# Output phase of a hybrid layer on Trainium2: product groups and small TensorE steps in a mixed order, column sums folded on GpSimd

## The chip, the cores and the metric

The kernel runs on one core of a Trainium2 chip. The metric is the device time of one launch in microseconds (us). A core has TensorE (PE), VectorE (DVE), ScalarE (ACT), GpSimd (POOL) and SyncE (SP, which here issues the DMA transfers). Each engine works through its own instructions in order; semaphores order the engines among each other.

## The reference, cut to what matters

The layer has eight phases, one after the other, each a block of its own: modulation, input projection, recurrence, attention, output, routing, experts, combination. Only the output phase is changed. For each of 2048 tokens it computes:

```python
o  = concat([rms_norm(r * gelu(g), gn_rnn), rms_norm(a, gn_attn)]) @ w_out   # 512 + 512 -> 1024
x1 = layer_norm(alpha * x + g1 * o, ln1_g, ln1_b)                            # post-norm
h2 = modulate(x1, shift, scale)                                              # second layer norm, scaled and shifted
logits = h2 @ [router_g, router_e] + bias                                    # 36 columns
```

`x1` and `h2` go to HBM for the later phases, the logits stay in SBUF. The gains `gn` and the gate `g1` are multiplied into the weight. The root mean square of each half is taken of its token, so it is applied to the finished product of that half, one factor per token for each.

## The kernel before, in words

The tokens are 16 tiles (`T_LAT`) of 128. The recurrence half arrives transposed (`yT`, 128 channels by 4 blocks of 128 tokens), the attention half by rows (`at`); TensorE transposes the latter. For float32 accuracy with float16 products every operand is split into a high and a low float16 part, and three products are summed: high x high, high x low, low x high (L1416 to L1418). One tile takes 8 groups `k` of 6 such matmuls (128x128 weights, 512 columns): groups 0 to 3 sum the recurrence half in PSUM banks 2 and 3, groups 4 to 7 the attention half in banks 4 and 5.

At the start ScalarE rounds the weight to `whi` in 8 pieces (L1349), VectorE computes `wlo` (L1284), and TensorE starts when all 8 are there (L1387). Then `tiles` (L1193) gives each engine the same order of steps; step `t` is

- `project(t)`: TensorE's 48 product matmuls;
- `normalise(t - 1)`: ScalarE scales the recurrence half (L1373, to `t0`), VectorE adds the other half and the residual (L1312, L1314) and does two layer norms (L1315 to L1338), in which GpSimd twice raises a variance to the power -0.5 (L1275) while VectorE waits;
- `prepare(t + 1)`: ScalarE squares both halves (L1355, L1358) and rounds them (L1361 `yhi`, L1363 `ahi`), VectorE computes the low parts (L1292 `ylo`, L1294 `alo`), TensorE transposes the attention half (L1394) and sums the squares of the recurrence half over the channels by four matmuls with a column of ones (L1401), ScalarE copies that sum (L1365), VectorE scales it (L1298) and GpSimd takes the power (L1269);
- `route(t - 2)`: TensorE transposes `h2` in 8 blocks (L1428), ScalarE evicts them in two halves (L1381), TensorE multiplies by the router (8 float32 matmuls of 36 columns, L1434), VectorE adds the bias (L1342).

`yhi`, `ylo`, `ahi` and `alo` have one buffer each, so their writers wait until the products of the tile before have ended (`o_mm`, L1360 and L1291). The column sums lie in bank 0, which the transposes of `h2` write too: these wait for ScalarE's copy of the sum (L1424). SyncE loads `yT` and `at` of tile `t + 2` when the parts of tile `t` are made, stores `x1` and `h2` of tile `t`, and loads `x` (`xt`) of tile `t + 2`. `link` (L1305) makes VectorE wait for each own instruction; `v` counts 14 per tile.

## Time and profile before

| | us |
|---|---|
| median of 3 runs | 2208.11 |
| lowest, highest | 2204.58, 2208.21 |
| profiled execution, its span | 2208.1 |
| output phase, first ScalarE instruction to last logits | 848.5 to 1158.0 |
| busy over the whole span | PE 84%, DVE 68%, ACT 47%, POOL 18% |

The span is the profiled execution's own time; nothing of it lies outside. Starts are in us from the start of the span. The output phase lies in slices 16 to 21 of the page's 40. A matmul's duration includes its way through the array, so matmuls overlap, and what one costs is the distance to the next start. In the lists "xN" is the number of instructions merged into a row, and a bracket gives the engine's idle time just before it and what ended that.

### The profile page before, as it was taken

To read this page: it belongs to the slowest core of one execution; us is meant where nothing else is said; L and a number is where in the kernel's file an instruction comes from. 1 tells how busy PE (TensorE), PEld (TensorE's weight loads), DVE (VectorE), ACT (ScalarE), POOL (GpSimd) and SP (SyncE) were. 2 spreads that over 40 slices of the span, in tenths; PEclk is the share of its full clock that TensorE was granted. 3 is DMA by queue.
4 is the path that set the end of the run, shared out by engine and by line. 5 is a ranking of instruction groups with operands and counts; after the bars stand their busy time and mean duration, and the time that the engine had idled before them with its cause. 6 is when DMAs were issued, how large, how long until landed. Compare 5 with 4: busy or idle time off the path is not lost. (4 is left out here: it accounts for less than half of the span.)

```text
span 2208.1 us, 41507 instructions
## 1 busy us (share of the span) xinstructions
PE 1847.0 (84%) x11836; PEld 1047.0 (47%) x11837; DVE 1498.4 (68%) x1859; ACT 1036.7 (47%) x1360; POOL 388.5 (18%) x375
## 2 busy tenths in 40 slices
PE   2488988889489996999971799999999988989946
PEld 0066666534277774555540345455444444445422
DVE  2357676388789995777669626656758888765537
ACT  1044434577478885222210514544646766543326
POOL 0000000000012211222212112222322323222213
PEclk7689999999799997988975799999999999999979
DMA  9712121276351111333323738778879999986637
GB/s 369 290 58 96 57 85 58 106 246 230 134 196 57 62 52 58 124 114 122 124 77 118 267 67 282 221 225 291 295 230 375 377 370 379 329 285 179 213 83 266
DMA packets 167722, 417.63 MB, mean 189 GB/s; under 512 B 16160, under 2 KB 24768, under 8 KB 163952
## 3 DMA queue, kind: packets, MB, share of 16 engines
q1 hardware_dynamic: 152832, 362.87, 44.9%
q0 software_dynamic: 14832, 54.01, 10.0%
q8 instruction: 34, 0.56, 0.1%
q14 instruction: 24, 0.20, 0.0%
HBM read 343.39 MB, written 73.45 MB: 189 GB/s over the span
## 5 line engine op out<-in xcount | busy, mean ns | idle before, releaser
L1946 PE MATMUL ps<-arena 128*128 x1200 | 459.3, 383 | 43.3 <-DVE arena L1866 43.1
L1866 DVE SCALAR_TENSOR_TENSOR arena<-arena 128x2048 f32 (+1 forms) x186 | 421.1, 2289 | 107.3 <-ACT arena L1810 49.9
L1947 PE MATMUL ps<-arena 128*128 x1200 | 458.9, 382 | 0.0
L1948 PE MATMUL ps<-arena 128*128 x1200 | 458.5, 382 | 0.0
L1804 ACT ACTIVATE arena<-arena 128x2048 f32 (+1 forms) x124 | 233.2, 1908 | 154.1 <-DMA arena<-w 67.9
L618 PE MATMUL ps<-arena 128*128 128x256 f16 (+1 forms) x1680 | 237.7, 303 | 21.1 <-DVE arena L503 21.1
L618 PEld LDWEIGHTS ps<-arena 128*128 128x128 f16 x1680 | 165.8, 100 | 87.3 <-DVE arena L503 15.2
L1946 PEld LDWEIGHTS ps<-arena 128*128 128x128 f16 x1200 | 118.1, 98 | 185.2 <-issue 59.5
L1948 PEld LDWEIGHTS ps<-arena 128*128 128x128 f16 x1200 | 118.4, 99 | 140.7 <-issue 4.5
L1947 PEld LDWEIGHTS ps<-arena 128*128 128x128 f16 x1200 | 118.1, 98 | 131.8 <-issue 4.0
L1810 ACT ACTIVATE arena<-arena 128x2048 f32 (+1 forms) x62 | 117.4, 1908 | 68.7 <-DMA arena<-w 50.6
L1866 DVE SCALAR_TENSOR_TENSOR arena<-ps,arena 128x512 f16<-128x512 f32 (+1 forms) x101 | 96.4, 954 | 70.4 <-ACT arena L1827 44.2
L1105 DVE CUSTOM_DVE_ANT_0 arena<-ps,arena,small 128x640 f32<-128x640 f32 x128 | 112.8, 881 | 14.4 <-PE ps L1047 5.5
L1047 PE MATMUL ps<-arena 128*128 (+3 forms) x768 | 94.0, 259 | 28.9 <-DMA arena<-qT_d 28.1
L1416 PE MATMUL ps<-arena 128*128 128x512 f16 x256 | 109.0, 426 | 2.9 <-ACT arena L1373 2.9
L1817 ACT ACTIVATE arena<-ps 128x1024 f16<-128x1024 f32 x51 | 52.0, 1019 | 122.8 <-PE ps L1941 122.8
L1059 PE MATMUL ps<-idn,arena 128*128 128x128 f32 x640 | 93.5, 277 | 18.8 <-ACT arena L1138 9.7
L1417 PE MATMUL ps<-arena 128*128 128x512 f16 x256 | 108.7, 425 | 0.0
L1418 PE MATMUL ps<-arena 128*128 128x512 f16 x256 | 107.9, 421 | 0.0
L1138 ACT ACTIVATE arena<-arena,small 128x640 f32<-128x640 f32 x128 | 105.0, 820 | 6.2 <-DVE small L1105 6.2
L1147 ACT ACTIVATE arena<-ps 128x640 f16<-128x640 f32 x128 | 90.1, 704 | 35.7 <-PE ps L1078 30.9
L1111 DVE SCALAR_TENSOR_TENSOR arena<-ps,arena 128x640 f16<-128x640 f32 x128 | 104.8, 819 | 1.9 <-ACT arena L1147 1.9
(287 smaller groups left out, 3040.5 us busy)
## 6 DMA issues: line engine op xcount, KB each, us to landing
arena<-w SPq DMA_DIRECT2D x186, 1024.0 KB, 12.9
arena<-hT_d SPq DMA_DIRECT2D x64, 512.0 KB, 6.0
arena<-w_mod SPq DMA_DIRECT2D x12, 2048.0 KB, 17.2
h_d<-arena SPq DMA_DIRECT2D x17, 512.0 KB, 3.0
x_d<-arena SPq DMA_DIRECT2D x17, 512.0 KB, 2.6
arena<-x SPq DMA_DIRECT2D x8, 1024.0 KB, 6.3
hT_d<-arena SPq DMA_DIRECT2D x16, 512.0 KB, 3.7
arena<-x SPq DMA_DIRECT2D x16, 512.0 KB, 4.7
```

The lines of the kernel that those rows point to most:

```text
L618: mm = pe.matmul(o, lhs, rhs, start=first and n == 0, stop=last and n == 2)
L1105: nc.vector.tensor_tensor_reduce(b[f"s{m % 4}"], scores_at(m), b[f"mask{j}"], -undo, neg_sink[:, h:h + 1], ALU.add, ALU.min, nm[j][:, h:h ...
L1138: nc.scalar.activation(b[f"s{m % 4}"], b[f"s{m % 4}"], ACT.Exp, bias=nm[j][:, h:h + 1], scale=-1.0, accum_out=den[j][:, h:h + 1]).then_inc ...
L1416: pe.matmul(o, lhs_hi, whi[:, k0 + k, cols], start=(k == 0), stop=False)
L1417: pe.matmul(o, lhs_hi, wlo[:, k0 + k, cols], start=False, stop=False)
L1418: mm = pe.matmul(o, lhs_lo, whi[:, k0 + k, cols], start=False, stop=(k == C_RNN - 1))
L1804: nc.scalar.activation(part(buf, whi, n * PIECE, PIECE), b["st"][:, n * PIECE:(n + 1) * PIECE], ACT.Copy, scale=W_SCALE).then_inc(hi13, 1)
L1810: nc.scalar.activation(part(buf, whi, n * PIECE, PIECE), b["st"][:, n * PIECE:(n + 1) * PIECE], ACT.Copy, scale=W_SCALE).then_inc(hi2, 1)
L1866: return nc.vector.scalar_tensor_tensor(dst, src, scale, high, ALU.mult, ALU.subtract)
L1946: pe.matmul(out, high, part(buf, whi, at, 512), start=first, stop=False)
L1947: pe.matmul(out, high, part(buf, wlo, at, 512), start=False, stop=False)
L1948: return pe.matmul(out, low, part(buf, whi, at, 512), start=False, stop=last)
```

## The change

TensorE's small steps are put between the 8 product groups, and the two halves get semaphores of their own (`o_y`, `o_mm`). A step `t` of TensorE is now: group 0, transposes of `at` (t + 1), group 1, first half of the transposes of `h2` (t - 2), group 2, second half, column sum (t + 1), groups 3 and 4, first half of the router's matmuls (t - 2), group 5, second half, groups 6 and 7. GpSimd adds the four blocks of squares to one (`fold`, two additions of 256 and 128 columns), so that one matmul into bank 7 does the column sum. `yhi`, `ylo`, `ahi` and `alo` get two buffers each. VectorE computes the low parts of tile t + 1 and adds the router's bias between an instruction of `normalise` and its wait for GpSimd's power. TensorE waits for each piece of the split weight by itself, and tile 0 is prepared between the 4th and 5th piece. SyncE loads both first pairs of `yT` and `at` ahead of `xt`, and refills one tile further ahead. `fold_d` reuses a semaphore of the first phase, whose count is already 1.

```diff
-    b = arena_slices(arena[:, 0:OUT_W0], 0, [("logits", T_LAT * 36), ("ones", 1), ("mh", 2), ("ysq", 512), ("asq", 512)]
-                     + [(n, 256) for n in ("yhi", "ylo", "ahi", "alo")]
+    b = arena_slices(arena[:, 0:OUT_W0], 0, [("logits", T_LAT * 36), ("ones", 1), ("mh", 2), ("ysq", 512), ("ysum", 128), ("asq", 512)]
+                     + [(f"{n}{j}", 256) for n in ("yhi", "ylo", "ahi", "alo") for j in range(2)]
...
+            def refill(t, j):
+                sp.wait_ge(lo, START + 2 * t + 2)
+                sp.sem_inc(g["alone"], 1)
+                sp.wait_ge(sq, START + 2 * t + 2)
+                sp.sem_inc(g["alone"], 1)
+                load_in(t + 2, j)
+
+            refill(0, 0)
+            for t in range(T_LAT):
+                if t + 3 < T_LAT:
+                    refill(t + 1, 1 - t % 2)
+                stores(t, t % 2)
+                if t + 2 < T_LAT:
+                    load_x(t + 2, t % 2)
...
+            def fold(t):
+                pool.wait_ge(sq, START + 2 * t + 1)
+                pool.sem_inc(g["alone"], 1)
+                pool.wait_ge(ssm, START + t)
+                pool.sem_inc(g["alone"], 1)
+                nc.gpsimd.tensor_tensor(b["ysq"][:, 0:2 * P], b["ysq"][:, 0:2 * P], b["ysq"][:, 2 * P:4 * P], ALU.add).then_inc(fold_d, 1)
+                pool.wait_ge(fold_d, START + 2 * t + 1)
+                pool.sem_inc(g["alone"], 1)
+                nc.gpsimd.tensor_tensor(b["ysum"], b["ysq"][:, 0:P], b["ysq"][:, P:2 * P], ALU.add).then_inc(fold_d, 1)
+
+            def first():
+                fold(0)
+                prepare(0, 0)
+
+            def step(t, j):
+                if has_next(t):
+                    fold(t + 1)
+                if known(t, 1):
+                    normalise(t - 1, 1 - j)
+                if has_next(t):
+                    prepare(t + 1, 1 - j)
+            tiles(pool, first, step, lambda: normalise(T_LAT - 1, 1))
...
                 link(nc.vector.scalar_tensor_tensor(t1, t1, mv[:, 0:1], b["l1g"], ALU.subtract, ALU.mult))
+                if while_first is not None:
+                    while_first()
                 dve.wait_ge(pw, START + 2 * t + 1)
...
                 link(nc.vector.scalar_tensor_tensor(x1n, x1, mv[:, 0:1], b["sc2"], ALU.subtract, ALU.mult))
+                if while_second is not None:
+                    while_second()
                 dve.wait_ge(pw, START + 2 * t + 2)
...
+            def first():
+                nc.vector.tensor_scalar(b["sc2"], b["sc2"], 1.0, None, ALU.add).then_inc(w_ok, 1)
+                for k in range(C_RNN):
+                    split_w(k)
+                low_y(0, 0)
+                low_a(0, 0)
+                squares(0, 0)
+                for k in range(C_RNN, KD):
+                    split_w(k)
+                dve.wait_ge(w_ok, START + 1)
+
+            def step(t, j):
+                def first_wait():
+                    if has_next(t):
+                        low_y(t + 1, 1 - j)
+
+                def second_wait():
+                    if has_next(t):
+                        low_a(t + 1, 1 - j)
+                    if known(t, 2):
+                        route(t - 2)
+                if known(t, 1):
+                    normalise(t - 1, 1 - j, first_wait, second_wait)
+                else:
+                    first_wait()
+                    second_wait()
+                if has_next(t):
+                    squares(t + 1, 1 - j)
+
+            def finish():
+                normalise(T_LAT - 1, 1)
+                route(T_LAT - 2)
+                route(T_LAT - 1)
...
             def prepare(t, j):
                 act.wait_ge(in_ld[j], START + 32 * half(t) + 32)
 
-                act.wait_ge(ssm, START + t)
+                act.wait_ge(fold_d, START + 2 * t)
                 nc.scalar.activation(b["ysq"], b[f"yT{j}"], ACT.Square).then_inc(sq, 1)
 
-                act.wait_ge(ssv_d, START + t)
+                if known(t, 2):
+                    act.wait_ge(o_y, START + t - 1)
+                nc.scalar.activation(yhi[j], b[f"yT{j}"], ACT.Copy, scale=X_SCALE).then_inc(hi, 1)
+
+                if known(t, 2):
+                    act.wait_ge(ssv_d, START + t - 1)
+                act.wait_ge(sq, START + 2 * t + 1)
                 nc.scalar.activation(b["asq"], b[f"at{j}"], ACT.Square, accum_out=ss[j][:, 1:2]).then_inc(sq, 1)
-
-                act.wait_ge(o_mm, START + t)
-                nc.scalar.activation(yhi, b[f"yT{j}"], ACT.Copy, scale=X_SCALE).then_inc(hi, 1)
                 act.wait_ge(a_tr, START + t + 1)
-                nc.scalar.activation(ahi, ps[:, 6, :], ACT.Copy, scale=X_SCALE).then_inc(hi, 1)
+                if known(t, 2):
+                    act.wait_ge(o_mm, START + t - 1)
+                nc.scalar.activation(ahi[j], ps[:, 6, :], ACT.Copy, scale=X_SCALE).then_inc(hi, 1)
                 act.wait_ge(ssm, START + t + 1)
-                nc.scalar.activation(ss[j][:, 0:1], ps[:, 0, 0:1], ACT.Copy).then_inc(ss_d, 1)
-
-            def normalise(t, j):
-                act.wait_ge(o_mm, START + t + 1)
+                nc.scalar.activation(ss[j][:, 0:1], ps[:, 7, 64:65], ACT.Copy).then_inc(ss_d, 1)
+
...
+            def first():
+                for k in range(C_RNN):
+                    high_w(k)
+                prepare(0, 0)
+                for k in range(C_RNN, KD):
+                    high_w(k)
+
+            def step(t, j):
+                if has_next(t):
+                    prepare(t + 1, 1 - j)
+                if known(t, 2):
+                    route(t - 2)
+                scaled(t, j)
...
+            def column_sums(t):
+                pe.wait_ge(fold_d, START + 2 * t + 2)
+                pe.wait_ge(ss_d, START + t)
+                if known(t, 4):
+                    pe.wait_ge(lg, START + t - 3)
+                pe.matmul(ps[:, 7, 64:65], b["ysum"], b["ones"], start=True, stop=True).then_inc(ssm, 1)
+
+            def product(t, j, k):
+                bank, high, low, at = (2, yhi[j], ylo[j], k) if k < C_RNN else (4, ahi[j], alo[j], k - C_RNN)
+                if at == 0:
+                    pe.wait_ge(lo, START + 2 * t + (1 if bank == 2 else 2))
 
                     if bank == 2:
                         pe.wait_ge(o_act, START + t)
-                    elif not isinstance(t, int) or t > 0:
+                    elif known(t, 1):
                         pe.wait_ge(v, START + NV * t - NV + 1)
-                    for k in range(C_RNN):
-                        for n in range(2):
-                            o, cols = ps[:, bank + n, :], slice(n * 512, (n + 1) * 512)
-                            lhs_hi, lhs_lo = high[:, k * P:(k + 1) * P], low[:, k * P:(k + 1) * P]
-                            pe.matmul(o, lhs_hi, whi[:, k0 + k, cols], start=(k == 0), stop=False)
-                            pe.matmul(o, lhs_hi, wlo[:, k0 + k, cols], start=False, stop=False)
-                            mm = pe.matmul(o, lhs_lo, whi[:, k0 + k, cols], start=False, stop=(k == C_RNN - 1))
-                mm.then_inc(o_mm, 1)
-
-            def route(t, j):
-                pe.wait_ge(v, START + NV * t + 14)
-
-                pe.wait_ge(ss_d, START + t + 4 if not isinstance(t, int) else START + min(t + 4, T_LAT))
-                pe.wait_ge(h_ev, START + 2 * t)
+                if not known(t, 1):
+                    pe.wait_ge(w_lo, START + k + 1)
...
+            def router(t, n):
+                pe.wait_ge(h_ev, START + 2 * t + n + 1)
+
+                if n == 0:
+                    pe.wait_ge(lg, START + t)
+                    pe.wait_ge(ss_d, START + (min(t + 4, T_LAT) if isinstance(t, int) else t + 4))
...
+            def first():
+                pe.wait_ge(p_ok, START + 2)
+                transposes_a(0, 0)
+                column_sums(0)
+
+            def step(t, j):
+                product(t, j, 0)
+                if has_next(t):
+                    transposes_a(t + 1, 1 - j)
+                product(t, j, 1)
+                if known(t, 2):
+                    transposes_h(t - 2, j, 0)
+                product(t, j, 2)
+                if known(t, 2):
+                    transposes_h(t - 2, j, 1)
+                if has_next(t):
+                    column_sums(t + 1)
+                product(t, j, 3)
+                product(t, j, 4)
+                if known(t, 2):
+                    router(t - 2, 0)
+                product(t, j, 5)
+                if known(t, 2):
+                    router(t - 2, 1)
+                product(t, j, 6)
+                product(t, j, 7)
+
+            def finish():
+                for t in (T_LAT - 2, T_LAT - 1):
+                    for n in range(2):
+                        transposes_h(t, t % 2, n)
+                    for n in range(2):
+                        router(t, n)
```

## Rows read from the trace of the kernel before

**Rows 1.** The page's slices: granted TensorE clock, tenths of full speed.
```profile
PEclk7689999999799997988975799999999999999979
```

**Rows 2.** Waits in the output phase, 880 to 1125: us in total, times, longest.
```profile
ACT arena L1361 <- PE ps L1418: 118.8, 14, 11.3
...
DVE arena L1342 <- PE ps L1434: 39.4, 13, 3.4
```

**Rows 3.** TensorE in time over one step: start, length, line, shape, count, idle before.
```profile
974.78 0.60 PE L1394 MATMUL ps<-idn,arena 128*128 128x128 f32 x4
975.22 0.95 PE L1401 MATMUL ps<-arena 128*128 128x1 f32 x8
976.51 1.09 PE L1428 MATMUL ps<-idn,arena 128*128 128x128 f32 x8 [0.34 <-ACT small L1365]
978.41 1.97 PE L1434 MATMUL ps<-arena 128*128 128x36 f32 x16 [0.81 <-ACT arena L1381]
980.21 0.38 PE L1416 MATMUL ps<-arena 128*128 128x512 f16 x1
...
984.06 0.38 PE L1417 MATMUL ps<-arena 128*128 128x512 f16 x1
...
992.26 0.60 PE L1394 MATMUL ps<-idn,arena 128*128 128x128 f32 x4
```

**Rows 4.** Attention, and one output step: us, busy per engine, PEclk, DMA.
```profile
680.00:720.00 40.00, 36.53 (x574) 30.93 (x573) 37.16 (x70) 33.57 (x70) 10.79 (x11) 1.00 0.19 64
974.78:992.26 17.48, 16.33 (x85) 9.15 (x84) 12.60 (x19) 4.62 (x9) 3.90 (x4) 0.90 0.35 120
```

**Rows 5.** ScalarE in time: the first act behind a tile's products, twelve steps apart.
```profile
903.54 0.63 ACT L1361 ACTIVATE arena<-arena 128x512 f16<-128x512 f32 x1 [4.85 <-PE ps L1418]
...
1116.18 0.63 ACT L1361 ACTIVATE arena<-arena 128x512 f16<-128x512 f32 x1 [8.41 <-PE ps L1418]
```

**Rows 6.** VectorE in time over one step.
```profile
909.11 0.20 DVE L1342 TENSOR_TENSOR arena<-ps,arena 128x36 f32 x1 [1.86 <-PE ps L1434]
909.22 1.27 DVE L1312 SCALAR_TENSOR_TENSOR arena<-ps,small,arena 128x1024 f32<-128x1024 f32 x1
...
915.70 1.29 DVE L1325 SCALAR_TENSOR_TENSOR arena<-arena,small 128x1024 f32<-128x1024 f32 x1 [0.61 <-POOL small L1275]
...
920.71 1.29 DVE L1338 SCALAR_TENSOR_TENSOR arena<-arena,small 128x1024 f32<-128x1024 f32 x1 [0.53 <-POOL small L1275]
922.20 0.69 DVE L1292 SCALAR_TENSOR_TENSOR arena<-arena 128x512 f16<-128x512 f32 x1 [0.21 <-ACT arena L1363]
922.81 0.68 DVE L1294 SCALAR_TENSOR_TENSOR arena<-ps,arena 128x512 f16<-128x512 f32 x1
```

**Rows 7.** GpSimd by line and shape: count, busy us, mean ns.
```profile
L1027 POOL TENSOR_TENSOR arena<-arena 128x1024 f32 x8 | 19.0, 2371 | 2.8 <-DMA arena<-router 2.8
...
L1269 POOL TENSOR_TENSOR small<-small,arena 128x2 f32<-128x2 f32 x16 | 11.3, 704 | 73.8 <-DVE small L1298 73.8
```

**Rows 8.** The line L1105 alone: duration ns min, median, max.
```profile
L1105 DVE CUSTOM_DVE_ANT_0 arena<-ps,arena,small x128: 873/883/886, 611.2 to 838.4; 128x640 f32<-128x640 f32 x128
```

**Rows 9.** The phase's start: DVE, SP and PE in time.
```profile
849.76 9.66 DVE L1284 SCALAR_TENSOR_TENSOR arena<-arena 128x1024 f16<-128x1024 f32 x8 [0.56 <-ACT arena L1349]
...
848.90 0.50 SPq L1227 DMA_DIRECT2D arena<-attn_d  x1
...
859.52 1.09 PE L1394 MATMUL ps<-idn,arena 128*128 128x128 f32 x4 [14.45 <-DVE arena L1284]
...
861.96 0.59 PE L1416 MATMUL ps<-arena 128*128 128x512 f16 x1
```

**Rows 10.** DMA issues, 847 to 862: KB each, median us to landing.
```profile
arena<-attn_d SPq DMA_DIRECT2D x2, 256.0 KB, 4.9
```

**Rows 11.** First tile's end (875.27), and the phase's end, in time.
```profile
875.27 0.60 PE L1394 MATMUL ps<-idn,arena 128*128 128x128 f32 x4
...
1135.00 1.04 PE L1428 MATMUL ps<-idn,arena 128*128 128x128 f32 x8
...
1138.97 1.27 DVE L1312 SCALAR_TENSOR_TENSOR arena<-ps,small,arena 128x1024 f32<-128x1024 f32 x1
...
1157.84 0.20 DVE L1342 TENSOR_TENSOR arena<-ps,arena 128x36 f32<-128x36 f32 x1 [6.15 <-PE ps L1434]
```

More of the change, by code:

```diff
@@ L1191, in phase_output, with tiles @@
     NV = 14
-    def tiles(eng, prepare, project, normalise, route):
-        def step(t, j, first=False, second=False, last=False):
-            project(t, j)
-            if not first:
-                normalise(t - 1, 1 - j)
-            if not last:
-                prepare(t + 1, 1 - j)
-            if not first and not second:
-                route(t - 2, j)
-        prepare(0, 0)
-        step(0, 0, first=True)
-        step(1, 1, second=True)
+    def tiles(eng, first, step, finish):
+        first()
+        step(0, 0)
+        step(1, 1)
         with eng.Fori(1, T_LAT // 2 - 1) as i:
@@ L1209, in tiles, with known, has_next @@
         step(T_LAT - 2, 0)
-        step(T_LAT - 1, 1, last=True)
-        normalise(T_LAT - 1, 1)
-        route(T_LAT - 2, 0)
-        route(T_LAT - 1, 1)
-    def none(t, j):
-        pass
+        step(T_LAT - 1, 1)
+        finish()
+    def known(t, low):
+        return not isinstance(t, int) or t >= low
+    def has_next(t):
+        return not isinstance(t, int) or t + 1 < T_LAT
     def half(t):
@@ L1439, with finish @@
+            def finish():
+                for t in (T_LAT - 2, T_LAT - 1):
[3 more added lines that the diff above has]
+                        router(t, n)
+            tiles(pe, first, step, finish)
 W13 = 2 * KD * D_EXP
```

98 lines of the change are left out of this document (47 added, 51 removed).

## The prediction

> **What bounds the kernel now.** The change touches the output phase only, so I read that stage and not the whole span. The page's slices come first: in the 16th to 21st slice, 828 to 1159 us, the granted TensorE clock is 7, 9, 8, 8, 9 and 7 tenths, where the four slices of attention before them have 9 [rows 1]. Then the waits of the stretch: the longest is ScalarE's, 118.8 us for the end of a tile's products, and VectorE's is 39.4 us for the router's matmuls [rows 2]; TensorE waits little. So TensorE's own sequence sets the step. Third, TensorE in time [rows 3], read by the distances of starts, since the lengths overlap:
>
> - transposes of `at`: 974.78 to 975.22, 0.44 us, 0.11 each;
> - column sums (8 passes in 0.95) and the wait for ScalarE's copy (0.34): to 976.51, 1.29 us;
> - transposes of `h2` and the wait for ScalarE's eviction (0.81): to 978.41, 1.90 us;
> - router: to 980.21, 1.80 us;
> - 48 products: to 992.26, 12.05 us. The last 38 of them, from 984.06, take 8.20 us, 0.2158 each; the first ten take 3.85 us where 2.16 would do. The clock has gone to its lower level (1.2 GHz) behind the small steps and comes back after 3.4 us: 1.69 us lost.
>
> Together 17.48 us. Over twelve steps ScalarE's marker moves from 903.54 to 1116.18, 17.72 us a step [rows 5]; the 0.24 more is steps in which the low level lasts longer. VectorE is busy 12.6 us of a step, ScalarE 4.6, GpSimd 3.9, and the clock is 0.90 [rows 4].
>
> **The new step on TensorE.** 48 products at 0.2158: 10.36. Transposes of `at` 0.44. Column sum: 2 passes in place of 8, 0.22. Transposes of `h2`: 8 at 0.11, 0.88. Router 1.80. Sum 13.70; a step now returns five times from float32 pieces to products, before once. No row shows a return by itself (that behind the router is inside its 1.80, for 16 passes, 0.11 each, as for the transposes), so I bound one by 0 and 0.1 and take 0.1 for all: 13.8 us. That holds if both waits go and the clock stays up.
>
> The waits: the transposes of `h2` no longer share bank 0 with the sum, and between each transposition and its use stand two to three groups of 1.29 us, for ScalarE's copy and two evictions. The router's first half comes 2.6 us behind the column sum; ScalarE needs a copy and one eviction in that time, and is busy 4.6 us of a step in all [rows 4]. No wait is left there.
>
> The clock: attention's TensorE stream is a mix of transposes and short matmuls at 91% busy (36.53 of 40 us), and has 1.00 [rows 4]. The new step has no idle gap, and no small piece longer than 0.9 us between products. I take 1.00.
>
> **The other engines.** VectorE becomes the nearest rival. From L1312 at 909.22 to the end of L1338 at 920.71 + 1.29 = 922.00 a `normalise` takes 12.78 us [rows 6]. Two waits for GpSimd lie in it, 0.61 and 0.53. In the first goes `low_y` (0.61 from start to start), at no cost; in the second `low_a` (about 0.6) and the router's bias (0.11 to the next start), 0.2 more than the gap. The scaling of the squares (0.16) and the waits at the step's end add 0.4. That is 13.4 us, below 13.8, so TensorE still sets the pace, by 0.4 us only. The bias add waits for the router's second half, at 6 x 1.29 + 0.44 + 0.88 + 0.22 + 1.80 = 11.1 us of TensorE's step; VectorE comes to it at 920.71 - 0.53 - 909.22 = 11.0, plus 0.6 for `low_a`, 11.6. Behind it are queued L1338 and the next tile's normalisation; TensorE needs that `h2` only two steps on.
>
> GpSimd: nothing here shows a 256-column addition. 1024 columns of the same kind take 2371 ns, 2 columns of a power 704 [rows 7]. By columns the fold is 384/1024 of 2371, 0.9 us, plus a start for each and the wait between them: 1.3 us. Its bounds are 0.9 and 2 x 2.37 = 4.7. It starts when the power of tile t is done, about 0.8 us into TensorE's step, and the column sum needs it at 5.2 (three groups, all transposes but none of the router). So up to 4.4 us cost nothing; at 4.7 TensorE would stand 0.3 us a step. The power for `normalise` is asked for as L1321 starts, 915.70 - 0.61 - 1.28 - 909.22 = 4.6 us behind L1312 [rows 6], when a fold of 1.3 us is long over.
>
> The fold runs beside L1312 and L1314. L1105 has a maximum of 886 ns against a median of 883 over 128 instances [rows 8], though eight of GpSimd's 2.4 us multiplications ran in that stretch [rows 7]: no slowing. It reads one operand from PSUM, however, and L1314 has both in SBUF. The Trainium skill ("GPSIMD Engine Reference", section 8, Key points) says that GpSimd shares its SBUF interfaces with VectorE, with contention where a VectorE instruction has two SBUF inputs. By that rule L1314 could stretch; the rows don't show that case, and it is a rival below.
>
> SyncE: its transfers keep size and number; `yT` and `at` are now issued one step earlier, 13 us or more ahead of use.
>
> **The start.** Before, TensorE waits for the eighth low piece (849.76 + 9.66 = 859.42), and the first product starts at 861.96 [rows 9]. Now four pieces (VectorE at 854.6) and tile 0's parts are enough. `at` of tile 0 is issued at 848.90 and lands 4.9 us later [rows 9, 10], 853.8; square 0.6, fold 1.3, the column sum at the low clock 0.4: the first product at 856.1, 5.8 us earlier. Tile 0's products then include tile 1's transposes and sum, 1.2 us at the low clock. The end of tile 0 moves from 875.27 [rows 11] to 875.27 - 5.8 + 1.2 = 870.7. The later low pieces come every 1.2 us and are ahead of groups of 1.3 to 2.6 us.
>
> **The sum.** Step 1 has no `h2` yet: 11.0 us, to 881.7. Steps 2 to 14: 13 x 13.8 = 179.4, to 1061.1. Step 15 has no next tile: 13.1, to 1074.2. Before, that point is 1135.00 [rows 11]. The last `normalise` no longer waits for a router product (before it starts 4.0 us behind, at 1138.97), but VectorE gets to it just then, 1074.3. From there to the last logits nothing changes: 1138.97 to 1158.04 is 19.1 us [rows 11], so 1093.4 in place of 1158.0. The gain is 64.6 us: 4.6 at the start, 56.2 in the steps, 3.8 at the end. The profiled execution has 2208.1 us, the same as the median of the runs, so 2208.1 - 64.6 = 2143.5, say 2144 us.
>
> **The rivals.**
>
> - *VectorE sets the pace.* For: only 0.4 us of room, more waits of its own, and L1314 beside the fold. If L1314 (1.2 us) doubled, a step is 14.6: 0.8 x 13 = 10 us, 2154. Against: L1105 is unmoved [rows 8]. 18%.
> - *The clock still falls.* TensorE goes back and forth between float16 groups and float32 pieces five times a step, which no row shows, and rows 3 show that small steps of 5.4 us cost it the full clock. If it stays as before, 1.69 + 0.24 us a step over 14 steps: 27 us, 2171. The Trainium skill ("TensorE: Matmul & The Clock Gate", "A second HAM failure mode") tells of a kernel whose short idles between groups of matmuls made the clock oscillate; this is that mechanism. Against: attention's 1.00. 13%.
> - *The early start fails.* ScalarE's late pieces stand behind tile 0's fold and sum; if that chain is late by more than the pieces' lead, most of 4.6 us goes: 2148. 6%.
> - *The fold closes a loop, slower than before.* VectorE's squares, GpSimd's power, fold, column sum, ScalarE's copy, squares: TensorE, in order, stands in front of its fourth group until the fold is there. The fold has 4.4 us before it costs anything. To give back the 3.9 us of a step it must take 8.3 us; with the clock falling in those gaps (1.9 a step) 6.4 us would do. At 9 us the steps are 18.4: 2144 + 13 x 4.6 = 2204, and with the clock 2228. The nearest row, 2371 ns for 1024 columns, speaks against it. 4%.
> - *The steps are no shorter*, since something unseen orders them (a buffer, the wait of the bias add): within 0.2% of before. 3%.
>
> **How the numbers follow.** The forecast has 56%, 2138 to 2149 by itself: 2138 is steps of 13.4 us (0.4 x 13 = 5 less), 2149 has 0.1 us for each of five returns (0.4 x 13 = 5 more). The range reaches up through VectorE's case and part of the clock's: 2137 to 2162. About 0.2% (4.4 us) is what a measurement of this kernel can tell from no change. Faster 0.93, same 0.03, slower 0.04.
>
> **What would show it.** L1394's successor starting every 13.8 us; granted clock 1.00 in the phase and no ten slow products in a step; no wait of TensorE for ScalarE; VectorE busy over 90% of a step without waiting for GpSimd's power; GpSimd's two additions at 1.3 us together, and L1314 at 1.23 us beside them; the first product at 856; the last logits at 1093. Wrong: steps above 14.6 us, a clock near 0.9, or TensorE waiting for the fold.

## The result, and the profile after

The changed kernel takes 2148.1 us (median of 4 runs, 2146.1 to 2150.7), the kernel before 2206.5 in the same comparison: the ratio is 0.973, with a 95% interval of 0.972 to 0.975. The forecast was 2144, with 2137 to 2162 as its range. The medians differ by 58.4 us. The forecast's gain of 64.6 misses that by 6, and its time by only 4, since it was taken off 2208.1. The profiled execution has a span of 2144.2 us and a run's time of 2146.1: some 2 us lie outside the span in this and in every later run, though the text ahead says that nothing does.

All starts below are in us from the start of a span, and each kernel reaches the output phase at a slightly other moment, so I cut the phase by marks that both traces have. It begins with ScalarE's first weight piece and ends with VectorE's last bias add, and the starts of VectorE's first and last `normalise` divide it. All four marks are starts. The last column is worked out from the points that the forecast names: 870.7, 1074.3 and 1093.4.

| | before | after | gain | forecast |
|---|---|---|---|---|
| phase begins | 848.5 | 847.3 | | |
| to the first `normalise` | 29.4 | 23.5 | 5.9 | 7.2 |
| 15 steps | 261.1 | 206.7 | 54.4 | 57.5 |
| to the last bias add | 18.9 | 18.0 | 0.9 | 0 |
| whole phase | 309.4 | 248.2 | 61.1 | 64.6 |

The spans differ by 63.9: 61.1 in the phase, 1.2 ahead of it and 1.6 behind. So nearly the whole gain is in the phase. Each column is one profiled execution, while the medians are of four runs each, and their interval allows a gain of 55.8 to 62.4; so the table is for where the time went, and not for a check of the total. The sums can be off by 0.1 from rounding.

The page's granted clock, in tenths, which answers to [rows 1]: the 16th to 20th slice have 8, 9, 9, 9 and 9. Asked for by itself, the stretch from 861 to 1082 has 1.00.

```profile
PEclk7789999999979998999955999999999999999979
```

The waits of the stretch 870 to 1080 (who waits, for whom, total, times, longest). Against [rows 2], ScalarE's wait for TensorE is down from 118.8 to 71.4 us, and VectorE's of 39.4 for the router is gone. What is left for VectorE is many small ones, and TensorE now has one for GpSimd:

```profile
ACT arena L1430 <- PE ps L1476: 71.4, 14, 5.5
...
PE ps L1484 <- POOL arena L1285: 3.0, 6, 0.6
...
DVE arena L1311 <- DVE arena L1346: 2.5, 12, 0.2
DVE arena L1317 <- DVE arena L1359: 2.4, 12, 0.2
...
DVE small L1322 <- DVE arena L1367: 2.3, 12, 0.2
...
DVE arena L1337 <- issue: 2.0, 5, 0.4
```

One of these the forecast had named as a sign of being wrong: TensorE waits for the fold (L1484 for L1285), six times and 3.0 us in all. It fills time in which TensorE would wait for VectorE anyhow: e2 below keeps the fold, and TensorE has no such wait there.

Two steps, cut at VectorE's L1337, in windows (length, then busy time of PE, PEld, DVE, ACT and POOL, granted clock, DMA share, GB/s), against [rows 4]. The clock is 1.00 where it was 0.90. A step takes 13.94 and 14.13 us in place of 17.48.

```profile
939.96:953.90 13.94, 13.78 (x81) 8.02 (x79) 12.62 (x18) 4.73 (x9) 4.73 (x5) 1.00 0.43 150
953.90:968.03 14.13, 13.58 (x79) 8.05 (x78) 12.41 (x18) 4.71 (x9) 5.98 (x6) 1.00 0.43 148
```

VectorE in time over the first of them (start, length, line, idle before), against [rows 6]. The two waits for GpSimd's power, 0.61 and 0.53, are gone: L1311 and L1317, the low parts, stand in them. In front of both, of L1322 and of L1339 is an idle 0.2, and in front of L1337 in every second step 0.41 in which the profile shows nothing waited for.

```profile
939.96 1.28 DVE L1337 SCALAR_TENSOR_TENSOR arena<-ps,small,arena 128x1024 f32<-128x1024 f32 x1 [0.41 <-issue]
941.42 1.43 DVE L1339 SCALAR_TENSOR_TENSOR arena<-arena 128x1024 f32<-128x1024 f32 x1 [0.18 <-DVE arena L1337]
...
946.26 0.69 DVE L1311 SCALAR_TENSOR_TENSOR arena<-arena 128x512 f16<-128x512 f32 x1 [0.21 <-DVE arena L1346]
...
951.54 0.69 DVE L1317 SCALAR_TENSOR_TENSOR arena<-ps,arena 128x512 f16<-128x512 f32 x1 [0.20 <-DVE arena L1359]
...
953.72 0.17 DVE L1322 TENSOR_SCALAR small<-small 128x2 f32<-128x2 f32 x1 [0.19 <-DVE arena L1367]
953.90 1.28 DVE L1337 SCALAR_TENSOR_TENSOR arena<-ps,small,arena 128x1024 f32<-128x1024 f32 x1
955.37 1.23 DVE L1339 SCALAR_TENSOR_TENSOR arena<-arena 128x1024 f32<-128x1024 f32 x1 [0.18 <-DVE arena L1337]
```

GpSimd in time: the first fold, and the folds of those two steps. L1282 is the addition of 256 columns, L1285 that of 128.

```profile
852.32 2.19 POOL L1282 TENSOR_TENSOR arena<-arena 128x256 f32<-128x256 f32 x1 [4.94 <-ACT arena L1417]
...
940.40 0.73 POOL L1282 TENSOR_TENSOR arena<-arena 128x256 f32<-128x256 f32 x1
941.31 0.46 POOL L1285 TENSOR_TENSOR arena<-arena 128x128 f32<-128x128 f32 x1 [0.18 <-POOL arena L1282]
...
955.66 1.25 POOL L1285 TENSOR_TENSOR arena<-arena 128x128 f32<-128x128 f32 x1 [0.18 <-POOL arena L1282]
```

Read the pairs together. In one step GpSimd's L1285 starts at 941.31, ahead of VectorE's L1339 at 941.42, and L1339 takes 1.43 us. In the next, L1339 starts first (955.37), takes its 1.23, and L1285 behind it takes 1.25 in place of 0.46. Whoever comes first delays the other. So the fold takes 1.37 us in one step and 2.17 in the next.

TensorE in time in tile 14, which answers to [rows 3]. The pieces stand between products, and the distance from start to start is what each costs: the column sum 0.25, half a router product 0.82. A group of four transposes has 0.60 in this row, since the column sum behind it stood for the fold; in most steps it has 0.44. The products keep their pitch of 0.216 right behind every piece.

```profile
1054.30 0.60 PE L1511 MATMUL ps<-idn,arena 128*128 128x128 f32 x4
1054.90 0.38 PE L1484 MATMUL ps<-arena 128*128 128x1 f32 x2
1055.15 0.38 PE L1500 MATMUL ps<-arena 128*128 128x512 f16 x1
1055.36 0.38 PE L1501 MATMUL ps<-arena 128*128 128x512 f16 x1
...
1057.73 0.98 PE L1521 MATMUL ps<-arena 128*128 128x36 f32 x8
1058.55 0.38 PE L1500 MATMUL ps<-arena 128*128 128x512 f16 x1
```

The start, TensorE and then VectorE, against [rows 9, 11]. The first product starts 8.4 us into the phase; before it was 13.5.

```profile
855.20 0.59 PE L1484 MATMUL ps<-arena 128*128 128x1 f32 x2 [3.22 <-POOL arena L1285]
855.64 0.59 PE L1500 MATMUL ps<-arena 128*128 128x512 f16 x1
```

```profile
848.45 4.88 DVE L1304 SCALAR_TENSOR_TENSOR arena<-arena 128x1024 f16<-128x1024 f32 x4 [0.47 <-ACT arena L1411]
...
870.80 1.28 DVE L1337 SCALAR_TENSOR_TENSOR arena<-ps,small,arena 128x1024 f32<-128x1024 f32 x1 [6.21 <-PE ps L1502]
...
1077.45 1.28 DVE L1337 SCALAR_TENSOR_TENSOR arena<-ps,small,arena 128x1024 f32<-128x1024 f32 x1
```

### The profile page after: what moved, and what is told of

Read it like the earlier page. It is cut to its first block and busy times, and to the rows that moved or that the text cites. A ratio compares the mean times of both kernels' runs of the same rounds, so it can differ in the third digit from the quotient of the medians.

```text
span 2144.2 us, 41310 instructions
## 1 busy us (share of the span) xinstructions
PE 1797.0 (84%) x11738; PEld 1025.2 (48%) x11741; DVE 1498.0 (70%) x1859; ACT 1038.7 (48%) x1360; POOL 425.3 (20%) x407
## 5 line engine op out<-in xcount | busy, mean ns | idle before, releaser
L2025 DVE SCALAR_TENSOR_TENSOR arena<-ps,gslot,arena 128x1024 f32<-128x1024 f32 x50 | 64.0, 1280 | 62.0 <-PE ps L2070 46.0
L1896 POOL DMA_INDIRECT x_d<-arena,ix x50 | 94.7, 1894 | 41.8 <-POOL ix L1892 39.2
L1892 POOL COPY ix<-gidx 128x1 int32 (+1 forms) x50 | 28.1, 562 | 363.6 <-DVE arena L2025 363.6
```

The lines of the kernel that those rows point to most:

```text
L1896: pool.indirect_dma_start(g["x1_d"], bass.IndirectOffsetOnAxis(ix[:, 2:3], 0), b["y0"], None, compute_op=ALU.add)\
```

## The experiments

My theory after the result: VectorE, not TensorE, sets the step, since its waits inside the hardware loop cost more than I counted. The rival is that TensorE still does, with an unseen cost of its five returns to products. "Phase" is measured as above; after has 248.2. The ratios are to the kernel before, on the same chip. A phase is that of the profiled execution alone: e5's was the fastest of its four runs, 5 us below its median, and e8's 3 us.

| | median us | ratio (95%) | phase | against after |
|---|---|---|---|---|
| after | 2148.1 | 0.973 (0.972 to 0.975) | 248.2 | |
| e1_unroll_all | 2139.8 | 0.971 (0.969 to 0.972) | 240.3 | -7.9 |
| e2_unroll_dve | 2140.2 | 0.970 (0.968 to 0.972) | 240.5 | -7.7 |
| e3_no_fold | 2144.9 | 0.973 (0.971 to 0.974) | 246.8 | -1.4 |
| e4_pe_blocks | 2154.3 | 0.977 (0.975 to 0.979) | 254.3 | +6.1 |
| e5_blocks_no_fold | 2161.6 | 0.980 (0.978 to 0.982) | 265.4 | +17.2 |
| e6_fold_only | 2200.3 | 0.997 (0.996 to 0.999) | 301.9 | +53.7 |
| e7_late_fold_unroll | 2137.0 | 0.969 (0.967 to 0.970) | 237.8 | -10.4 |
| e8_slow_fold | 2158.8 | 0.979 (0.977 to 0.980) | 257.6 | +9.4 |
| e9_dve_order | 2153.3 | 0.977 (0.975 to 0.979) | 254.2 | +6.0 |
| e10_late_start | 2151.6 | 0.976 (0.975 to 0.978) | 252.2 | +4.0 |

### e1_unroll_all and e2_unroll_dve: who sets the step

Steps 2 to 13 are written out instead of looped: in e1 on every engine, in e2 on VectorE alone. The instructions and their order are the same.

```
-        with eng.Fori(1, T_LAT // 2 - 1) as i:
-            step(2 * i, 0)
-            step(2 * i + 1, 1)
+        for t in range(2, T_LAT - 2):
+            step(t, t % 2)
```

> The changed kernel with steps 2 to 13 of the output phase written out on every engine, in place of a hardware loop of six rounds. In the changed kernel VectorE's step is 14.04 us in the loop and 13.02 us in step 14, which is written out. Theory V (VectorE sets the pace of the looped steps, and about 1 us a step of it is waits whose counts come from the loop's register): VectorE's step falls to 13.0 to 13.2 us, TensorE with 13.55 to 13.7 us sets the pace, 12 x 0.4 = 4 to 6 us faster than the changed kernel, about 2143. Theory T (TensorE sets it, as forecast): within 1 us of the changed kernel. Theory G (fold, column sum and port hold both engines at 14): within 1 us as well, with TensorE's waits for GpSimd unchanged.

> The same, but written out on VectorE alone; the other engines keep their loop. V: nearly the whole gain of the full unrolling, 4 to 6 us. If the loop's cost sits on TensorE, GpSimd or ScalarE instead: less than 2 us.

Both shorten the phase by the same 7.7 to 7.9 us: VectorE's loop is the whole of it. VectorE in time in e2: the step is 13.18 us, for 14.04 in after's loop (the mean of 13.94 and 14.13, which alternate; all 12 looped steps average 14.01).

```profile
939.25 1.28 DVE L1341 SCALAR_TENSOR_TENSOR arena<-ps,small,arena 128x1024 f32<-128x1024 f32 x1
952.43 1.28 DVE L1341 SCALAR_TENSOR_TENSOR arena<-ps,small,arena 128x1024 f32<-128x1024 f32 x1
```

TensorE repeats its sequence every 13.44 us in e1 and e2 alike. The transposes of `at` of two neighbouring tiles in e1, and its window from 900 to 1050, with TensorE busy without a break:

```profile
949.47 0.60 PE L1475 MATMUL ps<-idn,arena 128*128 128x128 f32 x4
...
962.90 0.60 PE L1475 MATMUL ps<-idn,arena 128*128 128x128 f32 x4
```

```profile
900.00:1050.00 150.00, 150.00 (x870) 89.68 (x869) 140.96 (x204) 51.99 (x103) 65.18 (x56) 1.00 0.45 155
```

The gaps are gone line by line. From L1346 to L1311 it was 1.50 us from start to start, from L1359 to L1317 1.48, from L1367 to L1322 1.47 and from L1337 to L1339 1.47; in e2 these are 1.32, 1.32, 1.31 and 1.32. That is 0.65 a step, and with the 0.40 of every second step 0.85: the whole of 14.04 - 13.18.

The trace of after also has what VectorE's sequencer did, and it says where these come from. In the loop every count of a wait is worked out in a register, 12 times a step for `link` alone (L1332). Where such a wait comes by itself, the instruction behind it starts no later than in e2 (L1345 to L1346 0.19 us in both, L1352 to L1353 1.31 in both). The 0.16 is lost in the four places where a second wait with a worked-out count stands behind that of `link` and the engine has nothing queued: the register operation of L1308 starts at 946.1, when L1346 has just ended, and L1311 at 946.26. The 0.4 in front of L1337 is the loop's jump back, once for two steps. The profile calls it "issue", since it is no wait; the branch and the register operations behind it are here, in the gap between L1322 at 967.46 and L1337 at 968.03 (duration ns min/median/max, first and last start):

```profile
L1200 DVEq COMPARE_BRANCH  x1: 56/56/56, 967.6 to 967.6; - x1
L1200 DVEq FUSED_REGOPS  x1: 63/63/63, 967.8 to 967.8; - x1
```

So 13.44 is what TensorE's sequence costs (forecast 13.8, or 13.7 without a price for the returns), and the rival falls. The gain was larger than I expected, since TensorE's 13.44 was below my estimate. In the first half of the steps VectorE still takes 13.18: its first step of 12.9 us stands beside a TensorE step without `h2`, of 10.93, so it falls 2 us behind TensorE and has caught up only by the 8th step.

### e3_no_fold: the four matmuls of the column sum again, in after's order

```
-                pe.matmul(ps[:, 7, 64:65], b["ysum"], b["ones"], start=True, stop=True).then_inc(ssm, 1)
+                for c in range(C_RNN):
+                    mm = pe.matmul(ps[:, 7, 64:65], b["ysq"][:, c * P:(c + 1) * P], b["ones"], start=(c == 0), stop=(c == C_RNN - 1))
+                mm.then_inc(ssm, 1)
```

> The changed kernel without the fold: four column-sum matmuls of the squares again, inside the mixed order; GpSimd has only its powers. TensorE's step grows by 6 passes, 0.66 us, from 13.55 to 14.2. V: VectorE's 14.04 loses the 0.2 us that the fold costs it in every other step, TensorE now sets the pace: 0.15 x 13 = 2 us slower than the changed kernel, about 2150. T: 0.66 x 13 = 8 to 9 us slower, 2157. G: 1 to 2 us faster, since the fold goes. At the start the first product should be about 2 us earlier, since the fold's first addition takes 2.19 us beside VectorE's weight pieces; this can take 1 to 2 us off in all cases.

The first `normalise` starts 20.8 us into the phase, not 23.5: 2.7 us gained, because at the start TensorE had waited 3.22 us for a fold of 2.19 + 0.45. The steps lose 1.2 us in all (mean 13.86 against 13.78): TensorE now repeats every 14.11 us, 0.67 more than in e1, and sets the pace. VectorE's instruction that was L1339 is 1.23 us throughout. Beside the loop of VectorE the fold is thus a net loss of 1.4 us, and the ratios of e3 and after (0.973 both) can't tell this from nothing. It isn't worthless by itself: with VectorE written out, 14.11 against 13.44 would be an estimated 0.67 x 13 = 9 us, but no run has the one without the other.

### e4_pe_blocks: TensorE in blocks again, the rest as in after

```
-                product(t, j, 0)
+                for k in range(KD):
+                    product(t, j, k)
...
+                    for n in range(2):
+                        transposes_h(t - 2, j, n)
+                    for n in range(2):
+                        router(t - 2, n)
```

> The changed kernel with TensorE's steps in blocks again: 48 products, then transposes, column sum, transposes of h2, router, without pieces between. Buffers, fold and the other engines' orders stay. If the mixed order's worth is the clock: the lower level returns for 3.4 us or more a step (1.7 to 1.9 us lost) and a wait for ScalarE's eviction of 0.8 us, so a step of 16.0 to 16.3 us in place of 14.04: 25 to 30 us slower than the changed kernel, about 2175. Rival (the clock came from the removed waits and the shorter column sum, not from the mixing): the clock stays up, a step of 14.3 to 14.5: 4 to 6 us slower, about 2153.

The mixed order is worth 6.1 us beside VectorE's loop, not the 27 that its clock was to bring. TensorE's step in blocks is 14.14 and 14.22 us in turn, so against the 13.44 of e1 the order would be worth more; no run has that. TensorE in time, from the last product of a tile to the first of the next:

```profile
997.26 0.38 PE L1502 MATMUL ps<-arena 128*128 128x512 f16 x1
997.48 0.60 PE L1476 MATMUL ps<-idn,arena 128*128 128x128 f32 x4
997.91 0.28 PE L1484 MATMUL ps<-arena 128*128 128x1 f32 x2
998.05 1.07 PE L1511 MATMUL ps<-idn,arena 128*128 128x128 f32 x8
999.45 1.97 PE L1521 MATMUL ps<-arena 128*128 128x36 f32 x16 [0.33 <-ACT arena L1448]
1001.25 0.38 PE L1500 MATMUL ps<-arena 128*128 128x512 f16 x1
```

The same work in one block takes 3.8 us with one wait of 0.33, and the product behind it has its full pace (0.38 long) at once. The window of 965 to 1050 has clock 1.00. In [rows 3] that block took 5.4 us with two waits, and ten slow products followed.

### e5_blocks_no_fold: blocks, and the four matmuls too

The edits of e3 and e4 together.

> TensorE's steps in blocks as in the run before this one, and the column sums by four matmuls without a fold. The stretch between two tiles' products is 3.8 us with the fold (clock stays at the upper level) and was 5.4 us in the kernel before (clock falls each step); here it is 3.8 + 0.66 = 4.4 us, with one short wait. Theory C (what costs the clock is how long TensorE goes without products, and how idle it is in that time; between 3.8 and 5.4 us lies the point): if 4.4 us is still short enough, TensorE's step is 14.5 us and the phase 3 to 5 us longer than with the fold, about 2157; if not, 16.2 us a step, about 2180. A step between the two would speak against C. In both cases the first product is some 2 us earlier than with the fold.

It came out between the expected cases. The block is 4.5 us in the steps that keep their clock. The clock falls twice between 900 and 1050, where it fell in every step before. One of those two, TensorE in time:

```profile
978.89 0.60 PE L1473 MATMUL ps<-idn,arena 128*128 128x128 f32 x4
979.32 0.95 PE L1482 MATMUL ps<-arena 128*128 128x1 f32 x8
...
981.61 2.71 PE L1520 MATMUL ps<-arena 128*128 128x36 f32 x16 [0.40 <-ACT arena L1445]
984.13 0.62 PE L1499 MATMUL ps<-arena 128*128 128x512 f16 x1
984.54 0.63 PE L1500 MATMUL ps<-arena 128*128 128x512 f16 x1
```

Here the router runs at 2.52 us start to start, in place of 1.80, and the products behind it at 0.43: the lower level. The mean granted clock of 900 to 1050 is 0.97. So in blocks the fold is worth 265.4 - 254.3 = 11.0 us. The clock is the smaller part of it: the three steps that its two falls touch are 5.0 us longer in all than the other steps' surplus over e4. The four matmuls' own length of 0.67 a step makes some 9, and the start, which has no fold to wait for, gives back 3.0. And e5 has neither the order nor the fold and is still 44.0 us below before. Of these, 8.4 lie ahead of the first `normalise`, 34.7 in the 15 steps and 0.8 behind the last. In a step the block is 5.4 us before and 4.5 here, with the same matmuls in it, so 0.9 of waits are gone, and the 48 products behind it take 10.36 in most steps, where they took 12.05. The 44 belong to what e5 has in common with after: two buffers for the parts, so that a tile's parts can be made while the products of the tile before still run; a bank of its own for the sum; each half of the router's work waiting for its own eviction; and VectorE's order and the early start, which e9 and e10 measure below.

### e6_fold_only: the kernel before, with the fold alone

```
-                for c in range(C_RNN):
-                    mm = pe.matmul(ps[:, 0, 0:1], b["ysq"][:, c * P:(c + 1) * P], b["ones"], start=(c == 0), stop=(c == C_RNN - 1))
-                mm.then_inc(ssm, 1)
+                pe.matmul(ps[:, 0, 0:1], b["ysum"], b["ones"], start=True, stop=True).then_inc(ssm, 1)
```

> The kernel before with the fold alone: GpSimd adds the four blocks of squares, one column-sum matmul; old order, single buffers, sum in bank 0, TensorE starts behind the eighth weight piece. The stretch without products falls from 5.4 to 4.8 us, two waits (0.34 and 0.81 us) stay in it. Theory C: if the clock still falls, a step of 17.1 us, 13 x 0.66 = 9 us faster than before, about 2197. If this is short enough for the clock, a step of 15.1 us, 30 to 35 us faster, about 2172. Rival (the double buffers and the order of VectorE and ScalarE bring the gain, not TensorE's stretch): the fold brings nothing or costs 1 to 2 us, since the sum then waits for GpSimd.

It gains 7.5 us in the phase. TensorE in time:

```profile
972.17 0.28 PE L1417 MATMUL ps<-arena 128*128 128x1 f32 x2
973.24 1.09 PE L1443 MATMUL ps<-idn,arena 128*128 128x128 f32 x8 [0.79 <-ACT small L1382]
975.14 1.97 PE L1449 MATMUL ps<-arena 128*128 128x36 f32 x16 [0.81 <-ACT arena L1398]
```

The sum is 0.7 us shorter (0.28 long against 0.95), and the wait for ScalarE's copy behind it has grown from 0.34 to 0.79: two thirds of the saving turned into a wait. The block is 5.2 us, and the clock of 900 to 1050 is 0.89: it falls in nearly every step, though not in the one shown. A shorter instruction in front of a wait on another engine gives back most of what it saves, which is why the fold needs the other edits to pay.

### e7_late_fold_unroll: the version that the first runs point to

VectorE is written out as in e2, and tiles 0 and 1 get their sums by four matmuls, the others by the fold.

```
-                pe.wait_ge(fold_d, START + 2 * t + 2)
+                if known(t, 2):
+                    pe.wait_ge(fold_d, START + 2 * t - 2)
+                else:
+                    pe.wait_ge(sq, START + 2 * t + 1)
```

> The changed kernel with VectorE's steps written out, and the sums of tiles 0 and 1 by four matmuls (GpSimd folds from tile 2 on, since its first addition takes 2.19 us beside VectorE's weight pieces and 0.73 later). Meant to beat both kernels. From the parts: VectorE written out shortened the phase from 248.2 to 240.5 us, no fold at the start shortened first weight piece to first normalisation from 23.5 to 20.8 us. If the two add: a phase of 237.8 us, 2.7 us faster than VectorE written out alone, about 2137. If the early start is taken back by something later (VectorE's weight pieces 4 to 7 are late then, or TensorE's pace absorbs it): within 1 us of 2140.

The phase is 237.8 us, and the median of 2137.0 (2135.6 to 2141.5, 5 runs) is below both kernels: 10.4 us less than after in the phase, of which e2 has 7.7 and the start 2.7. The two gains add up, which is what two separate causes do.

### e8_slow_fold: a fold that takes longer

From tile 2 on GpSimd does a multiplication of 1024 columns between the two additions, on a buffer that nothing else uses.

```
+                if known(t, 2):
+                    nc.gpsimd.tensor_tensor(b["idle"], b["idle"], b["idle"], ALU.mult)
```

> The changed kernel with a multiplication of 1024 columns on GpSimd between the two additions of each fold from tile 2 on, on data of its own that nothing uses: the fold takes 1.3 + 2.4 = 3.7 us or more in place of 1.3. This is the loop of the prediction's fourth rival (VectorE's squares, GpSimd's power, fold, column sum, TensorE's later groups, VectorE's next normalisation). Theory of the forecast: up to 4.4 us of fold cost nothing, so less than 2 us slower than the changed kernel. Theory of the port (GpSimd and VectorE instructions with two SBUF inputs exclude each other): the multiplication stretches beyond 2.37 us or VectorE's instructions beside it do, the sum is later than 5.2 us into TensorE's step, and steps grow by 0.5 to 2 us: 7 to 25 us slower.

It costs 9.4 us, where my forecast had called a fold of up to 4.4 us free; this one takes 4.0 to 4.2. GpSimd in time in two steps, then VectorE's line beside the first; L1342 is here what L1339 is in after:

```profile
974.02 1.89 POOL L1287 TENSOR_TENSOR arena<-arena 128x1024 f32<-128x1024 f32 x1 [0.18 <-POOL arena L1283]
...
989.80 2.69 POOL L1287 TENSOR_TENSOR arena<-arena 128x1024 f32<-128x1024 f32 x1 [0.18 <-POOL arena L1283]
```

```profile
974.13 2.86 DVE L1342 SCALAR_TENSOR_TENSOR arena<-arena 128x1024 f32<-128x1024 f32 x1 [0.18 <-DVE arena L1340]
```

GpSimd starts first at 974.02 and ends at 975.91; VectorE, 0.11 behind it, ends at 976.99, as if it had begun its 1.23 us only when GpSimd was almost done. In the other step VectorE starts first and GpSimd's instruction takes 2.69 in place of 1.89. Steps alternate between 15.4 and 14.2 us, 13.9 and 14.1 in after. So in this pair the two engines exclude each other for nearly the length of an instruction, and where VectorE sets the pace, its own delay is paid in full: 2.86 - 1.43 = 1.43 us, by which the long step is longer. GpSimd's delay in the other step costs 0.05.

### e9_dve_order: VectorE's old order

The low parts stand behind `normalise` again and the bias add behind them, so that no work fills VectorE's two waits.

```
-                    normalise(t - 1, 1 - j, first_wait, second_wait)
+                    normalise(t - 1, 1 - j)
...
+                    low_y(t + 1, 1 - j)
+                    low_a(t + 1, 1 - j)
```

> The changed kernel with VectorE's old order: low parts of tile t + 1, squares and the router's bias behind the whole normalisation, not in its two waits for GpSimd's power. TensorE's mixed order, fold and double buffers stay. Theory V (VectorE sets the pace of the loop): its step grows by the two waits it then has again, 0.61 + 0.53, less a few tenths, from 14.04 to about 15.0 us, 12 x 0.95 = 11 to 13 us slower than the changed kernel, about 2160. Rival (TensorE sets it and VectorE has slack): less than 2 us. Second rival (the low parts now come too late for TensorE's first group, which stalls and loses the clock): 15.5 us a step or more, 2167 and above.

It costs 6.0 us, half of what I expected. The steady step is 14.30 us against 14.04. Half of the 6.0 comes at the edges, 2.0 in the first two steps and 1.0 in the 14th. The waits for the power are back (0.54 and 0.53), and TensorE stands behind the late low part. The longest of these waits, 2.55 us ahead of 885.77, was followed by a granted clock of 0.50 from 887.1 to 890.5, in TensorE's mixed order. The same is seen once in e8, at 1023.3 behind a wait of 1.73. The waits of the stretch 900 to 1050 on VectorE, and of 870 to 1090 on TensorE:

```profile
DVE arena L1367 <- POOL small L1275: 5.3, 10, 0.5
DVE arena L1352 <- POOL small L1275: 4.8, 9, 0.5
```

```profile
PE ps L1492 <- DVE arena L1311: 10.1, 13, 2.5
```

Filling the two gaps gains less than their 1.07 us, since the filled version pays elsewhere. In after both low parts and L1322 have their 0.2 in front of them, the loop's jump adds 0.4 in every second step, and L1339 is delayed beside the fold; here of these only L1311 has its 0.2, nothing stands in front of L1337, and L1339 is 1.23 us.

### e10_late_start: TensorE waits for all eight low pieces

```
+                pe.wait_ge(w_lo, START + KD)
```

> The changed kernel, but TensorE waits for all eight low weight pieces before tile 0's first product, as in the kernel before. The eighth piece ends 14.7 us behind ScalarE's first one, the first product then starts some 6.3 us later than in the changed kernel (8.4 us behind it). If the early start is worth what it moves: 5 to 6 us slower, about 2154. If VectorE's work of tile 0 hides part of it (VectorE sets the pace from step 1 on, and its first normalisation starts when TensorE ends tile 0): the same 5 to 6 us, since that is a chain too. If the clock comes back at the same moment in both, up to 1 us less. Below 3 us the start would not have been on the path.

The phase is 4.0 us longer. TensorE in time:

```profile
862.30 0.61 PE L1500 MATMUL ps<-arena 128*128 128x512 f16 x1 [6.20 <-DVE arena L1304]
...
865.60 0.38 PE L1500 MATMUL ps<-arena 128*128 128x512 f16 x1
```

The first product starts 6.3 us later than in after, measured from the phase's start (14.7 against 8.4), but behind it the lower clock level lasts a shorter time: 3.3 us (862.30 to 865.60) against 4.6 in after (855.64 to 860.21). The products get part of the lateness back.

## Why the prediction was right, and where it was not

- **TensorE's step: right in kind, 0.36 too long.** The sum of its parts gave 13.8 us, and it measures 13.44 (e1). The allowance for the returns was not needed. In e1 the router's halves take 1.62 us where 1.80 was read from [rows 3], and the column sum 0.14 for 0.22; products and transposes have the distances that were taken.
- **The clock: right in value, wrong in reason.** It is 1.00, so the second rival (13%) fell. But I laid the old fall to the absence of products and credited the mixing with its end. In e4 nothing is mixed and it is 1.00 too, and in e9 everything is mixed and it falls once, behind a wait of 2.55 us. What e4 has in place of before is a block of 3.8 us for 5.4, shorter by waits and by the 0.7 of the sum. For the 0.7 an effect is shown, by e4 against e5, but it is two falls in the whole phase against none, and one trace of each; for the waits it is argued, since e5 differs from before in several edits. The oscillation that the Trainium skill tells of ("TensorE: Matmul & The Clock Gate", "A second HAM failure mode") isn't seen in after, mean clock 1.00 over 861 to 1082.
- **Who sets the pace: wrong.** The step that failed is "That is 13.4 us, below 13.8, so TensorE still sets the pace". VectorE's loop step is 14.04. Three terms were mis-sized. The low parts in the two waits were to cost nothing and 0.2; they cost 0.22 and 0.38, since each begins with a 0.2 of its own. "The waits at the step's end add 0.4" measured 0.57, with the loop's jump in it. L1339 beside the fold adds 0.1. The loop's whole price is 0.85 a step, a part of which was in my 12.78 without my seeing it. The trace of before has two of these already, which I passed over: between 880 and 1125 L1314 waits 0.2 behind L1312 in 12 steps, and up to 0.3 of "issue" stands before L1312 in five.
- **The first step: missed.** The sum has 11.0 us for step 1, "no `h2` yet". That is TensorE's share, and e1 has 10.93. But VectorE does its first whole `normalise` in it, and from its first to its second L1337 it takes 13.05. Where VectorE sets the pace, this counts.
- **The rival "VectorE sets the pace": right in its head, mis-sized in its cause.** It named L1339 (L1314 before) beside the fold, doubled. Measured is 1.43 for 1.23 in every second step, 0.1 a step on average; the loop does the rest. The evidence against it did not bear on the case, as the prediction half said: the unmoved L1105 [rows 8] reads one operand from PSUM, and e8 shows the effect where both are in SBUF, 2.86 for 1.23. By the rule of the Trainium skill ("GPSIMD Engine Reference", section 8, Key points) on instructions with two SBUF inputs, contention was to be expected here, and the traces agree (1.43 and 2.86 for 1.23).
- **The fold's cost: its size right in every second step, wrong at the start, and its room wrong.** It is 0.73 + 0.18 + 0.46 = 1.37 us against 1.3 taken, and 2.17 where VectorE's L1339 starts before its second addition. The first one runs beside VectorE's fourth weight piece and the low part behind it (L1304 and L1311), which have two SBUF inputs, and takes 2.19 + 0.18 + 0.45 = 2.8, 1.5 more, for which the first product waits. That "up to 4.4 us cost nothing" was worked out from TensorE's order alone. It left VectorE's port out, and e8 priced the omission at 9.4 us.
- **The start and the end.** The first product came 5.1 us earlier in the phase where 5.8 was forecast, though tile 0's parts were ready sooner and the fold later than I took. What it is worth by itself is 4.0 (e10), against 4.6. The end was taken as unchanged and came out 0.9 us shorter, 18.0 for 18.9.
- **The total: near, in part by luck.** It was 61.1 us in the phase for 64.6. In the 15 steps, where 3.1 are missing, two errors stand against each other. With VectorE out of the way (e1) the 15 steps take 198.8 us, 4.8 less than the forecast's 203.6, and VectorE's loop and first step put 7.9 on top. By steps: the first was 2.0 longer than forecast, the 12 looped ones 2.5 in all, the last two 1.4 shorter. Had I priced TensorE right and VectorE as I did, the forecast would have been 2139, 9 us below the result.

What stays open: how the 44 us of e5 divide among buffers, the sum's own bank, the split evictions, VectorE's order and the early start. (The 6.0 of e9 and the 4.0 of e10 were measured in after, not in e5.) A version with single buffers for the split parts was not tried, since in TensorE's new order ScalarE's copy of the sum would stand behind a part whose buffer comes free only behind the router that waits for that copy. Nor was the kernel before run with VectorE written out, though its trace has small waits of the same kind.

## What to carry to other kernels

When a clock falls behind a block of small matmuls, look first at the waits inside the block: the edits that take them out, with VectorE's order and the early start, stand behind most of this gain (44 of 61 us), the finer mixing behind 6. When two engines come within a few per cent of each other, count each idle tenth of a looped step on both, the jump back too, and write out the loop on the one that sets the pace. Work given to an idle engine isn't free by its idle time: look at which instructions of the pacing engine read from the same memory at that moment.

## What the runs showed of the hardware that I had not expected

- In a hardware loop on VectorE, a second wait with its count from the loop's register, standing behind a wait for the instruction just issued, costs some 0.16 us (four places a step), and the jump back 0.4 a round; such waits that stand alone cost nothing (L1345 to L1346 0.19 us looped and written out). Written out, both are gone (14.04 against 13.18 us for the same 18 instructions).
- GpSimd and a VectorE instruction with two SBUF inputs exclude each other almost whole: 1.23 becomes 2.86 us when started 0.11 behind a GpSimd instruction of 1.89, and GpSimd's 256 columns take 2.19 us instead of 0.73 behind a VectorE instruction of 1.28 and one of 0.69.
- Going back and forth between float32 pieces and float16 products five times a step costs TensorE nothing that shows: e1's 13.44 us are 48 products at 0.2158 and the pieces at their own distances (0.44, 0.88, 0.14 and 1.62), at clock 1.00.
- The clock can fall in a mixed order too: it was 0.50 for 3.4 us in e9 shortly behind a wait of 2.55 us, and in e8 behind one of 1.73.
